# A one-core hybrid decoder layer: all eight mixer steps in the order u, turn, gate tile, states, gates, z, diagonal

## The reference

```python
h = rms_norm(x, norm_mix)
proj = h @ w_in            # lru_x 1024 | lru_gate 1024 | ssd_z 1024 | ssd_xbc 2048 | ssd_dt 16
# RG-LRU group: u = causal conv of lru_x, two block-diagonal gates of u, a linear recurrence,
#   times gelu(lru_gate), then rms_norm
# SSD group: xbc = silu(causal conv), dt = softplus(...), 8 chunks of 128 tokens:
#   y = scores * decay @ xdt  (diagonal) + C @ state (carried over chunks) + xs * d
#   y = rms_norm(y * silu(ssd_z))
x = x + concat(y_lru, y_ssd) @ w_out
h = rms_norm(x, norm_ffn)
x = x + hier_moe(h)        # top-1 group of 4, top-2 of its 8 experts, SwiGLU of width 512
out = rms_norm(x, final_norm)
```

## Time and profile before

| | |
|---|---|
| median of 3 runs | 1537.78 us |
| the profiled execution's own time | 1537.96 us |
| its span, first to last instruction | 1536.1 us |
| mean granted TensorE clock | 0.945 |
| TensorE, DVE, ScalarE, POOL busy | 90%, 64%, 51%, 36% |

### The profile page before, as it was taken

One profiled execution on the slowest core, in us unless ns is written; L12 is line 12 of the kernel. 1 busy time (PEld: TensorE's weight loads), 2 busy tenths in 40 slices (PEclk: granted clock), 3 DMA queues, 4 the chain that ended last, 5 costly groups with the idle time before them and its releaser, 6 DMA issues.

```text
span 1536.1 us, 19669 instructions
## 1 busy us (share of the span) xinstructions
PE 1385.1 (90%) x6510; PEld 1141.5 (74%) x6510; DVE 977.0 (64%) x918; ACT 788.0 (51%) x845; POOL 551.6 (36%) x485
## 2 busy tenths in 40 slices
PE   6899999999999989869996289999999999999960
PEld 4688888888888867658785268888888888888750
DVE  5433333665555675631134659899999899999847
ACT  5232223455444355210033058888788888788844
POOL 1344445665556655846400411121121221121122
PEclk8999999999999999989997589999999999999985
DMA  4112112333332333423412259999999999999756
GB/s 164 42 45 75 50 48 62 100 107 106 93 93 75 101 94 143 144 76 101 144 69 96 98 190 389 384 377 376 373 382 384 384 386 375 395 382 398 271 197 271
DMA packets 99540, 308.68 MB, mean 201 GB/s; under 512 B 15648, under 2 KB 17568, under 8 KB 99360
## 3 DMA queue, kind: packets, MB, share of 16 engines
q1 hardware_dynamic: 89840, 291.17, 52.2%
q0 software_dynamic: 9648, 16.80, 3.0%
HBM read 293.62 MB, written 32.64 MB: 212 GB/s over the span
## 4 chain that ended last, share of the span: by engine, by line
PE 48%; DVE 7%; ACT 1%; DMA 1%; issue 1%; POOL 0%; DVEq 0%; ACTq 0%; POOLq 0%
PE ps L822 35%; PE ps L698 9%; PE ps L811 2%; DVE X L1539 2%; PE ps L774 1%; PE ps L842 1%; PE ps L803 0%; PE ps L765 0%; DVE YSL L1337 0%; DVE X L1358 0%; DVE late L1419 0%; DVE XBX L1332 0%; DMA ring_dn<-in_moe 0%; DMA late<-y_d 0%; DVE split_b L1480 0%
## 5 line engine op out<-in xcount | busy, mean ns | idle before, releaser
L1583 POOL TENSOR_TENSOR GH<-raw,ones 128x512 fp32r<-128x512 f32 x106 | 127.2, 1200 | 325.5 <-PE ps L551 269.5
L551 PE MATMUL ps<-XH,GH 128*128 128x512 f32 x656 | 208.9, 398 | 7.8 <-ACT M L968 5.4
L551 PE MATMUL ps<-XL,GH 128*128 128x512 f32 x656 | 205.7, 393 | 0.0
L551 PE MATMUL ps<-XH,GL 128*128 128x512 f32 x656 | 205.4, 392 | 0.0
L1585 POOL TENSOR_TENSOR GL<-raw,GH 128x512 fp32r<-128x512 f32 x106 | 156.6, 1477 | 8.3
L1480 DVE TENSOR_TENSOR split_c<-ring_gu,split_c 128x1024 fp32r<-128x1024 f32 x127 | 149.6, 1219 | 1.1 <-ACT split_c L1047 1.1
L551 PEld LDWEIGHTS ps<-XH,GH 128*128 128x128 f32 x656 | 122.9, 190 | 34.0 <-ACT M L968 5.6
L551 PEld LDWEIGHTS ps<-XH,GL 128*128 128x128 f32 x656 | 124.4, 190 | 26.5
L551 PEld LDWEIGHTS ps<-XL,GH 128*128 128x128 f32 x656 | 124.3, 190 | 26.3
L822 PE MATMUL ps<-split_c,XTH 128*128 128x512 f32 x520 | 140.5, 392 | 0.0
L1047 ACT ACTIVATE split_c<-ring_gu 128x1024 fp32r<-128x1024 f32 x130 | 130.1, 1050 | 1.7 <-PE ps L822 1.1
(11 more groups left out here) (286 smaller groups left out, 2874.1 us busy)
## 6 DMA issues: line engine op xcount, KB each, us to landing
ring_gu<-in_moe SPq DMA_DIRECT2D x264, 512.0 KB, 5.7
ring_dn<-in_moe SPq DMA_DIRECT2D x132, 512.0 KB, 6.4
raw<-in_win SPq DMA_DIRECT2D x82, 256.0 KB, 2.7
T<-acs_d SPq DMA_DIRECT2D x16, 512.0 KB, 4.6
raw<-in_wout SPq DMA_DIRECT2D x32, 256.0 KB, 2.7
T<-in_x SPq DMA_DIRECT2D x8, 512.0 KB, 6.8
X<-in_x SPq DMA_DIRECT2D x8, 512.0 KB, 3.3
h_d<-M SPq DMA_DIRECT2D x8, 512.0 KB, 2.6
```

The source lines that it names most:

```text
L551: mm = pe.matmul(ps[:, bank + h, :], wp[:, w, col], x[:, kk, h * 512:(h + 1) * 512], start=(kk == 0 and n == 0), stop=(kk == KT - 1 and n ...
L1583: link(pool, pool.tensor_tensor(hi, raw[:, r, :], one.to_broadcast([P, GR]), ALU.mult), g_hi, at + 1)
```

## The change

TensorE's mixer order becomes u, turn_chunk, g, states, gates, z, diagonal for all eight steps. `Z_LAST` is the number of the step from which this holds; it is 0, so every branch `i < Z_LAST` is empty. u goes to banks 0 and 1, g to 2 and 3, z to 4 and 5, the diagonal to 2 and 3. The gates make the input gate first. Each engine's and queue's list is put in the same order: z's silu and its store come at the end of a step, DVE does taps, chunk, state, scan, combine. POOL's list has the same form as before, but starts a tile later in `TILES`: `first_next` is the first granule of g 0.

At the beginning: one Sqrt of a constant ahead of the first square; ident and pv are issued before x tile 0; the dt granules' matmuls between the turns are 6, 6 and then 12 behind turn 7 (before 12 and 12 between them); cumulative sums and rows move one x,B,C tile back on TensorE, ScalarE and DVE.

In the output projection: DVE multiplies z of tile k+1 and weighs LRU part k+4 ahead of the low part of tile k, ScalarE weighs one part more ahead of its loop, POOL adds square k behind split k+2 (before k+3), and SP's list follows.

```diff
-for _i in range(KT - 1):
-    TILES += [("z", _i), ("u", _i), ("g", _i)]
-TILES += [("u", KT - 1), ("g", KT - 1), ("z", KT - 1)]
+Z_LAST = 0
+for _i in range(KT):
+    TILES += [(_n, _i) for _n in ("zug" if _i < Z_LAST else "ugz")]
...
-        x_bank = lambda i: 2 * (i % 2)
-        y_bank = lambda i: 2 - 2 * (i % 2)
-        first_next = AT["z", 0] + 2
+        x_bank = lambda i: 2 if i >= Z_LAST else 2 * (i % 2)
+        y_bank = lambda i: 0 if i >= Z_LAST else 2 - 2 * (i % 2)
+        first_next = 2 * (2 * KT + 2)
...
+            sp.dma_start(ident[:, :], a["ident"]).then_inc(const_in, 16)
+            sp.dma_start(pv[:, :], a["pv"]).then_inc(const_in, 16)
             x_tile(0)
-            sp.dma_start(pv[:, :], a["pv"]).then_inc(const_in, 16)
-            sp.dma_start(ident[:, :], a["ident"]).then_inc(const_in, 16)
...
-                if at == 10:
+                if at == 13:
                     sp.wait_ge(sp_exp, 5)
...
                 for n in range(2, 6):
                     after(at + n)
+                if i >= Z_LAST:
+                    sp.wait_ge(z_act, i + 1)
+                    sp.dma_start(z_d[i], TI).then_inc(z_out, 16)
...
-                after(N_GR + m)
-                if 4 <= m < 8:
-                    sp.wait_ge(accs, m - 3)
-                    z_rows(m - 1)
+                if m >= 2:
+                    after(N_GR + m)
+                if 2 <= m < 6:
+                    sp.wait_ge(accs, m - 1)
+                    z_rows(m + 1)
...
                 if t in (5, 6):
-                    granule_mms(t - 5, 4, (0,))
+                    granule_mms(0, 4, (0,), range(2 * (t - 5), 2 * (t - 4)))
+            granule_mms(1, 4, (0,))
             pe.wait_ge(xl_ready, TT)
...
-                elif j == 1:
+                elif j == 2:
                     pe.wait_ge(tri_in, 16)
                     pe.wait_ge(sp_arg, 2)
...
-                elif j == 2:
+                elif j == 3:
                     pe.wait_ge(sp_arg, 3)
...
-                    pe.wait_ge(yt_done, c)
                     pe.wait_ge(gate_act, 2 * c)
+                    if c <= Z_LAST:
+                        pe.wait_ge(yt_done, c)
+                    else:
+                        pe.wait_ge(z_act, c)
...
-                if i >= 1:
-                    pe.wait_ge(yo_used, i)
-                for g, bank in enumerate((6, y_bank(i))):
+                for g in (0, 1) if i < Z_LAST else (1, 0):
+                    bank = y_bank(i) if g else 6
+                    if g == 0 and i >= 1:
+                        pe.wait_ge(yo_used, i)
...
+            for i in range(Z_LAST, KT):
+                if i == 0:
+                    pe.wait_ge(cv_x, 16)
+                wait(pe, gate_act, 2 * i)
+                project(("u", i), y_bank(i))
+                turn_chunk(i)
+                wait(pe, g_act, i)
+                wait(pe, yt_done, i)
+                project(("g", i), x_bank(i))
+                states(i)
+                gates(i)
+                if i < KT - 1:
                     pe.wait_ge(st_upd, i + 1)
+                project(("z", i), 4)
+                pe.wait_ge(g_act, i + 1)
+                diagonal(i, 2)
...
             act.wait_ge(par_done, 1)
+            act.activation(stat[:, 6, 0:1], eps[:, 0:1], ACT.Sqrt)
...
+            for i in range(Z_LAST, KT):
+                lru_tap(i)
+                if i < KT - 1:
+                    turned_b(i)
+                decay_exp(i)
                 if i == KT - 1:
                     weigh_lru(0)
                     weigh_lru(1)
                 lru_gates(i)
-            z_tile(KT - 1, 4, KT)
-            square_lru(KT - 1)
+                z_tile(i, 4, i + 1)
+                square_lru(i)
             weigh_lru(2)
...
             deviation(slice(0, TT), 7, 1)
+            weigh_lru(3)
...
-                if k + 3 < KT:
-                    weigh_lru(k + 3)
+                if k + 4 < KT:
+                    weigh_lru(k + 4)
...
+            for i in range(Z_LAST, KT):
+                lru_taps(i)
+                chunk(i)
+                state(i)
+                if i == KT - 1:
+                    weigh_lru(0)
+                    weigh_lru(1)
+                lru_scan(i)
+                combine(i, 2)
...
+            weigh_lru(2)
+            times_z(0)
+            weigh_lru(3)
+            for k in range(KT):
+                if k + 1 < KT:
+                    times_z(k + 1)
+                if k + 4 < KT:
+                    weigh_lru(k + 4)
                 dve.wait_ge(ysh_act, k + 1)
-                dve.scalar_tensor_tensor(YSL[:, k, :], y, param("ssd_norm", k),
+                dve.scalar_tensor_tensor(YSL[:, k, :], XBX[:, k, :], param("ssd_norm", k),
...
+                for q in range(2):
+                    split(at + q)
+                    decays(i, q)
                 skip_term(i)
-                split(at)
+                split(at + 2)
                 if i >= 1:
                     add_squares(ACCL, AA, i == 1, sq_l, accl, i)
-                for n in range(1, 4):
+                for n in range(3, 6):
                     split(at + n)
...
-                if 3 <= m < 3 + KT:
-                    k = m - 3
+                k = m - 2
+                if k < KT:
```

More of the change, by code:

```diff
@@ L438, in _ @@
                 after(at)
-                sp.wait_ge(z_act, i + 1)
-                sp.dma_start(z_d[i], TI).then_inc(z_out, 16)
+                if i < Z_LAST:
+                    sp.wait_ge(z_act, i + 1)
+                    sp.dma_start(z_d[i], TI).then_inc(z_out, 16)
                 after(at + 1)
@@ L472, in _ @@
             lru_rows(6)
+            for n in range(4, 6):
+                after(at + n)
             sp.wait_ge(accl, 8)
@@ L541, in _, with granule_mms @@
         def _(pe):
-            def granule_mms(at, bank, halves):
+            def granule_mms(at, bank, halves, ks=range(KT // 2)):
                 q, w = at % 2, at % SPL
                 pe.wait_ge(g_lo, at + 1)
-                for k in range(KT // 2):
+                for k in ks:
                     col = slice(k * P, (k + 1) * P)
@@ L666, in diagonal @@
                 mm.then_inc(y_mm, 1)
[L668 to L675, removed]
+            for i in range(Z_LAST):
+                if i == 0:
+                    pe.wait_ge(cv_x, 15)
+                else:
+                    pe.wait_ge(gate_act, 2 * i)
+                project(("z", i), x_bank(i))
                 turn_chunk(i)
@@ L682, in _ @@
                 states(i)
-                if not last:
-                    pe.wait_ge(z_act, i + 1)
+                pe.wait_ge(z_act, i + 1)
                 project(("g", i), x_bank(i))
                 gates(i)
-                if not last:
+                pe.wait_ge(st_upd, i + 1)
+                diagonal(i, 4)
+            for i in range(Z_LAST, KT):
+                if i == 0:
+                    pe.wait_ge(cv_x, 16)
[8 more added lines that the diff above has]
+                if i < KT - 1:
                     pe.wait_ge(st_upd, i + 1)
[L689 to L692, removed]
+                project(("z", i), 4)
+                pe.wait_ge(g_act, i + 1)
+                diagonal(i, 2)
             def product(y, w, t, bank, at, first, last):
@@ L915, in _ @@
             conv_tile(1)
+            conv_tile(2)
             act.wait_ge(sp_arg, 4)
@@ L920, in _ @@
                            ACT.Exp).then_inc(sp_exp, 1)
-            conv_tile(2)
+            conv_tile(3)
             act.wait_ge(row_mm, 1)
@@ L924, in _ @@
             link(act, act.activation(ACS, pair(6)[0:NH, :], ACT.Copy), sp_exp, 5)
-            for j in range(3, KT):
+            for j in range(4, KT):
                 conv_tile(j)
@@ L950, in lru_gates @@
                 one = slice(i, i + 1)
-                act.wait_ge(gt_mm, 2 * i + 1)
                 wait(act, lru_g, i)
[L953 to L958, removed]
+                for n, g in enumerate((0, 1) if i < Z_LAST else (1, 0)):
+                    act.wait_ge(gt_mm, 2 * i + n + 1)
+                    if g == 1:
+                        act.wait_ge(z_out, 16 * (i + 1 if i < Z_LAST else i))
+                    link(act, act.activation(TI if g else TR, pair(y_bank(i) if g else 6),
+                                             ACT.Tanh, bias=prep[:, g, one], scale=0.5),
+                         gate_act, 2 * i + n + 1)
                 wait(act, accl, i)
@@ L980, in weigh_lru, with turned_b, lru_tap @@
                                scale=param("lru_norm", k)).then_inc(ylh_act, 1)
[L982 to L992, removed]
+            def turned_b(i):
+                act.wait_ge(ts_mm, i + 1)
+                wait(act, st_mm, i)
+                act.activation(BT.rearrange("p g n -> p (g n)"), ps[:, 6, :], ACT.Copy
+                               ).then_inc(bt_ready, 1)
+            def lru_tap(i):
                 act.wait_ge(g_used, AT["u", i] + 2)
@@ L997, in _ @@
                                ).then_inc(tap_u, 1)
```

(46 more changed lines are left out.)

## The result

The changed kernel takes 1512.34 us (median of 4 runs, 1510.92 to 1514.24) against 1538.78 for the kernel before beside it: ratio 0.9832, 95% interval 0.9813 to 0.9851. The profiled execution took 1514.24 us, its span is 1512.4 us. Against the profiled 1537.96 that is 23.7 us less; the prediction had 23.5. The profiled execution is the slowest of the four, and between the two medians are 26.4 us.

The account below looks back on a forecast made before the run. TensorE, busy 1385.1 of 1536.1 us, was taken as the bound, so its idle spots count: 1537.96 - 4.5 - 7.9 + 7.8 + 3.9 - 8.6 - 14.2 = 1514.5, as a median 1514.3 us. Range 1505 to 1526.

Parts of the forecast that it names:

- Beginning: Normalisation and dt granules: earlier ident and Sqrt table, 12 matmuls moved into TensorE's 2.4 us idle spot; 4.5 us won.
- 3 if the clock drops anyway: Lower gain, in us, given for the kernel's start, against 4.5 expected and 5 if all goes well.
- Cumulative sums: One x,B,C tile later, TensorE's 5.1 us wait for DVE's softplus chain and 2.8 us of low clock go: -7.9 us.
- Step 0: First mixer step: u now waits 5.4 us for tap set 16, plus 2.4 us of low clock: +7.8 us (5.4 to 8.5).
- Steps 0 to 6: Mixer: z starts 0.55 us late behind DVE's state update in seven steps, which covers the diagonal's gelu wait: +3.9 us.
- Step 7: Last mixer step: idle spots of 1.4 and 5.4 us and 1.85 us of low clock go: -8.6 us.
- Output projection: POOL, at 7.4 us a round, becomes the late one instead of DVE; weights 10 to 15 at full pace: -14.2 us.
- is not in the way: In the output projection, DVE's evacuation can start at about 651 us and doesn't delay TensorE.
- the best case of -21: Rival: POOL doesn't bind the output projection, which wins 21 us instead of 14.2, total 1507 us; chance 0.15.
- the mean round of before: Alternative POOL round in the output projection, 6.8 us with DVE 70% busy; the sum would be 2 us lower.
- all at their worst 1534: Whole kernel: time in us if all terms came out at their worst; all at their best give 1504.
- the softplus wait: Rival: the wait only moves, to the row transposes behind tile 3; its 7.9 us return, 1522 us; chance 0.06.

Follow-up runs that it names:

- the experiment: Changed kernel with the old beginning put back (x tile 0 first, no early Sqrt, 12 and 12 matmuls between the turns): 1517.64 us, ratio 0.9865.
- the experiment with the shorter low clock: Changed kernel with the cumulative sums back behind tile 1 and the rows behind tile 2: 1518.78 us, ratio 0.9877.
- tap set 15: Changed kernel, but the first u tile waits for tap set 15, the last that reads its bank, instead of 16: 1505.07 us, ratio 0.9783.
- the variant without decay: Changed kernel without the DVE instruction that multiplies the state by its decay in steps 1 to 6: 1513.75 us, ratio 0.9825.

## Why the prediction was right

Every large wait came and went where it was forecast, and the terms came out like this:
- *Beginning, -4.5.* The traces of before and after differ by 3.6 us, that of the changed kernel being the latest of its eleven starts: while the six matmuls behind turn 5 ran, the clock was 0.50 (24.00 to 28.20 us). The mean start of the new beginning and the experiment say -5. The step's mechanism holds, and its "3 if the clock drops anyway" was nearly drawn.
- *Cumulative sums, -7.9.* 8.1 in the two traces, 6.9 in the experiment with the shorter low clock. Nothing was late next.
- *Step 0, +7.8.* 8.4 up to the first diagonal. The wait of 5.32 us and its low clock are 8.0 of it, which went with tap set 15.
- *Steps 0 to 6, +3.9.* 4.2 in six steps and the rest of the 8.4, about 0.3, in step 0. The idle time was 0.4 and not 0.55, in six steps and not in seven, and 0.3 of slower start was not counted: two errors that cancel. That z's delay covers gelu is shown by the variant without decay.
- *Step 7, -8.6.* 8.4: waits of 6.8 us, and 1.6 for the clock where 1.85 was taken.
- *Output projection, -14.2.* 14.7 here, 13.5 in the mean of eight traces. POOL's split of weight 3 ends at 608.6 us and that of weight 8 so that TensorE starts it at 645.46; the prediction's 616.7 and 653.7, less the 7.6 us that everything stands earlier, are 609.1 and 646.1. DVE's evacuation begins at 643.30, forecast 651 less 7.6. It "is not in the way" by 1.4 us only, so the best case of -21 would have needed an earlier end of DVE's list as well.

What sized that last term is the length of POOL's instructions beside DVE. By the mean round of before the stage would have been 2 us shorter than predicted, and in none of the eight traces it is more than 0.5 shorter. The lock of the port that the Trainium skill describes ("SBUF — State Buffer", section "SBUF: two separate sides") is what the prediction rested this on. POOL's medians of 1.90 and 3.37 us, against 1.04 and 2.40 once DVE's list has ended, agree with "the other fully blocks".

That the total came within 0.2 us of the profiled execution is in part luck: its start is 1.8 us later than the mean and its projection 1.1 shorter, and 1.5 us come from stages that the change doesn't touch. The medians differ by 26.4, 3 us more than forecast. In the prediction's list of bounds, "all at their worst 1534" doesn't follow from its terms, which give 1532, or 1540 with the softplus wait; nothing rests on it.

What the prediction left unsaid is what the terms mean together: the change named in the title, the order of the steps, costs 4 us more than it wins (12.6 against 8.4), and the whole gain is the beginning's, the sums' and the projection's.

## What to carry to other kernels

Where one engine is busy for 90% of the span, write the change as a ledger of its idle spots, with the wait, the low clock behind it and the slower start as three prices, and look for spots that the new order opens: uniform steps removed one at the end and opened a dearer one at the front. A mixed order (old front, new end, `Z_LAST = 6`) had both advantages for one constant. When two engines take turns on a port, count for each the length of its neighbour's instructions, and write down when both lists end: here they ended within 0.3 to 1.4 us of each other. A shorter square, which both had waited for, freed 8.5 us; taking work from one of them alone freed nothing.

## What was not expected of the hardware

After the same idle spot of 5.1 us the low clock cost 1.7 us in one execution and 3.0 in another (granted 0.81 over 8.8 us, 0.67 over 9.2 us). Over a whole stage it adds up to more: the same projection took between 145.0 and 147.6 us in eight traces, and the same beginning between 33.1 and 36.4 in eleven. With single profiles, a difference of 3 us between two kernels can be within that. DVE's two-input instructions, 1.2 to 1.3 us when POOL is idle, took up to 3.4 us beside POOL's square, in the changed kernel too.
